# Last head group of the odd layer: VectorE's stick-breaking passes of a step moved directly behind the transposes' copies

## The reference

```python
def _sb_core(q, k, v, qpos, kpos):
    z = jnp.einsum('bqhd,bkhd->bhqk', q, k).astype(jnp.float32) * (SB_HD ** -0.5)
    valid = kpos[None, :] < qpos[:, None]
    log_beta = jax.nn.log_sigmoid(z)
    log_rem = jnp.where(valid, jax.nn.log_sigmoid(-z), 0.0)
    later = lax.cumsum(log_rem, axis=3, reverse=True) - log_rem
    a = jnp.where(valid, jnp.exp(log_beta + later), 0.0).astype(v.dtype)
    return jnp.einsum('bhqk,bkhd->bqhd', a, v)

def _odd_layer(x, pos, caches, prm):
    ...
    q, k, v, g = _split_cols(x @ w_in, (SB_W, SB_W, SB_W, SB_W))
    ...
    o = (o.reshape(b, s, SB_W) * jax.nn.silu(g)) @ w_out
    y = _layernorm(ALPHA * x + o, ln_g, ln_b)
    return y, (k, v)
```

## Time and profile before

| | |
|---|---|
| median of 3 runs | 814.35 us |
| profiled execution | 814.67 us, its span 812.9 us |
| PE busy | 784.4 us, 96% of the span |
| DVE busy | 549.3 us, 68% |
| ACT busy | 393.0 us, 48% |
| POOL busy | 184.9 us, 23% |
| mean granted TensorE clock | 0.995 of full speed |

### The profile page before, as it was taken

How to read it: one execution, slowest core, us unless ns; L and a number is a source line. 1 busy time by engine, 2 the same in 40 slices (tenths; PEclk the granted TensorE clock), 3 DMA queues, 4 the chain that set the end, 5 groups by cost and what they waited for, 6 DMA issues and landing times.

```text
span 812.9 us, 16632 instructions
## 1 busy us (share of the span) xinstructions
PE 784.4 (96%) x6396; PEld 685.5 (84%) x6396; DVE 549.3 (68%) x1087; ACT 393.0 (48%) x903; POOL 184.9 (23%) x262
## 2 busy tenths in 40 slices
PE   6999999999999999999999999999999999999996
PEld 5997799889879987778999998888988888777674
DVE  4576366656677668766933575786577777879778
ACT  3234533444444444431424555765667565677710
POOL 3120010000311232001340142233322343662002
PEclk9999999999999999999999999999999999999998
DMA  7632121211624355414143344334433444444113
GB/s 239 165 102 73 52 61 58 73 34 35 151 66 123 91 121 155 149 54 128 59 125 104 108 116 131 106 106 132 131 107 106 126 118 124 110 129 146 57 40 129
DMA packets 62284, 86.23 MB, mean 106 GB/s; under 512 B 7936, under 2 KB 47648, under 8 KB 62208
## 3 DMA queue, kind: packets, MB, share of 16 engines
q1 hardware_dynamic: 52832, 61.88, 25.3%
q0 software_dynamic: 9376, 23.29, 11.5%
HBM read 74.25 MB, written 10.90 MB: 105 GB/s over the span
## 4 chain that ended last, share of the span: by engine, by line
PE 78%; issue 9%; DVE 7%; ACT 3%; POOL 2%; DMA 1%; SPq 0%; DVEq 0%; ACTq 0%; POOLq 0%
PE turn L1000 27%; PE pair L1000 17%; PE value L1000 14%; PE proj L1000 12%; PE turn L1049 2%; DVE probs L1780 1%; POOL rstd L973 1%; PE turn L1223 1%; PE proj L1049 1%; PE value L1049 1%; PE proj L1223 1%; PE pair L1049 1%; PE value L1223 1%; DVE probs L1776 1%; DMA x_sb<-in_x_prompt_dram 1%
## 5 line engine op out<-in xcount | busy, mean ns | idle before, releaser
L1650 DVE TENSOR_TENSOR w_words<-stage,w_words 128x512 fp32r<-128x512 f32 (+1 forms) x136 | 91.8, 682 | 80.4 <-ACT w_words L1423 80.2
L1000 PE MATMUL turn<-w_words,xT_hi 128*128 128x256 f32 (+2 forms) x664 | 142.5, 311 | 1.0 <-DVE xT_lo L1655 0.7
L1000 PEld LDWEIGHTS turn<-w_words,xT_hi 128*128 128x128 f32 x664 | 107.5, 192 | 6.5 <-DVE x_sb L1912 1.5
L1000 PE MATMUL turn<-w_words,xT_lo 128*128 128x256 f32 (+2 forms) x340 | 102.7, 302 | 0.0
L912 POOL DMA_DIRECT2D k_c<-in_cache_sb_k_dram x128 | 82.6, 653 | 84.0 <-DVE k_cT L1764 79.7
L1423 ACT CAST w_words<-stage 128x512 fp32r<-128x512 f32 (+1 forms) x144 | 87.4, 616 | 27.4 <-DMA stage<-in_w_in_even_dram 12.8
L1000 PE MATMUL turn<-xT_hi,w_words 128*128 128x320 f32 x384 | 90.0, 314 | 0.0
L1000 PE MATMUL value<-w_words,xT_hi 128*128 128x256 f32 (+2 forms) x360 | 79.7, 315 | 1.0 <-DVE w_words L1650 1.0
L1000 PE MATMUL proj<-w_words,xT_hi 128*128 128x256 f32 (+2 forms) x384 | 75.7, 296 | 0.2 <-DVE uq L1856 0.2
L1000 PE MATMUL pair<-w_words,xT_hi 128*128 128x512 f32 (+2 forms) x272 | 71.6, 349 | 0.0
L1000 PEld LDWEIGHTS turn<-w_words,xT_lo 128*128 128x128 f32 x340 | 65.1, 191 | 2.6
(11 more groups left out here) (497 smaller groups left out, 1705.6 us busy)
## 6 DMA issues: line engine op xcount, KB each, us to landing
stage<-in_w_in_odd_dram SPq DMA_DIRECT2D x64, 256.0 KB, 2.8
stage<-in_w_in_even_dram SPq DMA_DIRECT2D x44, 256.0 KB, 2.9
k_c<-in_cache_sb_k_dram POOLq DMA_DIRECT2D x128, 64.0 KB, 2.4
v_c<-in_cache_sb_v_dram SPq DMA_DIRECT2D x32, 256.0 KB, 2.9
mlaK<-in_cache_diff_k_dram POOLq DMA_DIRECT2D x32, 128.0 KB, 4.2
mlaK<-in_cache_diff_v_dram SPq DMA_DIRECT2D x8, 512.0 KB, 5.1
stage<-in_w_out_even_dram SPq DMA_DIRECT2D x16, 256.0 KB, 2.7
stage<-in_w_out_odd_dram SPq DMA_DIRECT2D x16, 256.0 KB, 2.7
```

The source lines that it names most:

```text
L1000: return nc.tensor.matmul(o, l, r, start=first, stop=last)
L1650: v.tensor_tensor(piece(w_lo[:, sec % 2, words]), piece(stage[:, n % STAGES, :]), piece(w_hi[:, sec % 2, words].bitcast(F32)), ALU.subtrac ...
```

## The change

In `stick_pipeline`, for steps of the last group alone, the job `stick` is put directly behind the step's `turn` and `turn2`. Before it stood at the step's end, behind the cached keys, the further bundles, the products of `bsT` and `value`, and `weigh`.

```diff
@@ -159,6 +159,9 @@
                 jobs.append(("turn2", s))
         coming = [("cacheT",) + steps[j] + (k,) for j in samples for k in range(2)
                   if i == max([j - 2, 0] + [n for n in samples if n < j])]
+        early = now[1] == GROUPS - 1
+        if early:
+            jobs.append(("stick", now))
         for bundle in fill[1:]:
             jobs += coming[:1] + bundle
             coming = coming[1:]
@@ -171,7 +174,8 @@
                 later.setdefault(i + turns_on, []).append(job)
         if i >= 1:
             jobs.append(("weigh", steps[i - 1]))
-        jobs.append(("stick", now))
+        if not early:
+            jobs.append(("stick", now))
     return jobs
```

## The result

The changed kernel is slower. Its median over 20 runs is 816.37 us (813.85 to 821.84), beside 813.56 us (811.91 to 815.34) for the kernel before, also 20 runs: ratio 1.0041, interval 1.0027 to 1.0055. The forecast was 811.8 us with a range up to 814.2. It was counted from the median of three runs, 814.35, which lies 0.8 above that of the 20; a gain of 2.6 us was forecast and a loss of 2.8 was measured.

A forecast was written before the change was run, and what follows sets the result against it. TensorE, busy 96% of the span, was taken to lose time only to waits, mainly for late sticks, and its clock. Savings 0.4 + 1.8 + 1.6 + 0.2 - 1.4 = 2.6 us gave 811.8 us; 8-in-10 range 810.4 to 814.2.

The forecast's parts named there:

- Score of B(2,0), saves 0.4: TensorE's 1.19 us wait at this score: the stick of B(3,0) ends earlier, saving 0.38 us; the rest waits for the product.
- Score of B(3,1), saves 1.8: TensorE's 1.82 us wait at this score goes whole, since the stick of B(2,0) starts at 714.9 us.
- Clock, saves 1.6: Six blocks of tile 0, near 725 us: no clock fall, so 4.2 us instead of 5.8; bounds 0 and 1.6.
- Score of BS3, saves 0.2: This score no longer waits about 0.2 us for the stick of BS2, which now stands ahead of other work.
- Key loads, cost 0 (bounds 0 and 1.7): VectorE's key turn waits 0.3 us for BS3's loads without reaching TensorE; at worst 2.0, of which 1.7 would.
- Sums and products in the middle, cost 0: Tile 3's difference and gate products behind sticks still come ahead of TensorE; cost 0, bounds 0 and 1.
- Difference of tile 2, costs 1.4: Near 766 us this difference stands behind two sticks and ends 1.4 us later; TensorE's wait grows from 0.74 to about 2.1.
- slower: the half clock spreads: Rival, 8%: clock falls at new waits before short products; two falls give 816.6 us, three 818.2, old fall not avoided.

The follow-up runs named there:

- e8: Kernel before with only the stick of B(3,0) moved early: 816.76 us, ratio 1.0031 to the kernel before.
- e11: Kernel before with only the stick of B(3,0) early and three GpSimd weight splits beside its scans cut to 16 of 512 columns: 812.66 us, ratio 1.0001.
- e4: Kernel before with only the stick of B(2,0) moved early: 810.67 us, ratio 0.9969 to the kernel before.
- e9: Changed kernel with one more key load on GpSimd, into an unread buffer, at the start of the odd layer: 812.73 us in one execution.
- e1: Changed kernel, all eleven sticks early, with BS3's eight key loads issued by SyncE instead of GpSimd: 814.58 us, ratio 1.0020 to the kernel before.
- e7: Changed kernel with sticks of B(3,0), B(1,1), B(0,0) back at the step's end and BS3's key loads issued by SyncE: 809.57 us, ratio 0.9952 to the kernel before.
- e3: Changed kernel with sticks of B(3,0), B(1,1), B(0,0) back at the step's end, key loads still on GpSimd: 813.97 us, ratio 1.0005 to the kernel before.
- e10: Kernel before with only the sticks of B(1,1) and B(0,0) moved early: 814.25 us, ratio 1.0013 to the kernel before.
- e2: Kernel before, no stick moved, with BS3's eight key loads issued by SyncE instead of GpSimd: 813.01 us, ratio 0.9990.
- e5: Changed kernel with three small loads at the kernel's start issued by SyncE instead of GpSimd: 815.79 us, ratio 1.0033 to the kernel before.

## Why the prediction was wrong

Step by step, as the prediction had them:

- **"Score of B(2,0), saves 0.4"** failed, by the size of one term. The chain was right (stick, half products, value product, score, and the new wait falls on the value product) but the scans were put at 1.17 + 1.8 and took 4.47. Started from 0.98 us earlier, TensorE's value product was due at 708.4 and began at 709.81; the scans' 1.5 us account for it. The number was an average over two unlike instructions of one row of two. e8 and e11 show the cause: alone the stick costs 0.31% and brings the wait of 2.14, with the splits beside it narrowed neither is there. The Trainium skill, page "SBUF — State Buffer", section "Who interferes with whom", has such instructions exclude each other for a whole instruction. The trace agrees in part: scans and splits end by turns, 1.07 to 1.09 us apart, and two splits of each profile took 2.18 to 2.31 us where the third took 1.27. But the first scan of after had run 1.10 us of its 1.17 when the split began, and that it still took 2.29 doesn't follow from such exclusion. By that rule this term was to be about nothing, nearer than mine, and it was worse than nothing, since both scans of the early stick paid in full and before only one did.
- **"Score of B(3,1), saves 1.8"** held: 1.89, and e4 shows it by itself.
- **"Clock, saves 1.6"** held in the profile, 1.63. Against the median it was too much, as far as the clocks of the runs tell: of the 73 runs of the kernel before, 23 have a mean clock of 0.998 and average 812.7, so in about a third of its runs there was no such fall to save, or less of one. e4's 2.5 us, less than 1.8 + 1.6, goes the same way.
- **"Score of BS3, saves 0.2"** held in sign, 0.41.
- **"Key loads, cost 0 (bounds 0 and 1.7)"** failed, and above its upper bound: the two stretches that it delays grew by 2.95. The 1.6 us by which the loads go out sooner look right (1.7) by luck: 0.98 of them came from ahead of the change, and GpSimd's own two splits, from 723.20 to 726.53, held the loads longer than the key turns did (through at 725.99). Wrong was that the stand would come again as long as before. It grew by 2.2, because its end, as the packets show (e9), follows not the issue of the loads but their traffic. VectorE came to the turn at 735.81, as forecast (735.5), and waited 2.81 us where 0.3 and at worst 2.0 were forecast. e1 (keys gone, half of the loss gone) and e7 against e3 (0.53%) show the price.
- **"Sums and products in the middle, cost 0"** isn't contradicted: with the keys by SyncE (e1) TensorE waits for no sum or product of the middle.
- **"Difference of tile 2, costs 1.4"** held: 1.65 in the profile, 1.1 by e10. VectorE's row from the sum to the end of the difference was counted as 6.5 us and took 6.5 (759.81 to 766.31).
- **The rival "slower: the half clock spreads"** had 8%. It put two falls at 816.6 and the median is 816.37, but the nearness is luck. It kept the forecast's waits and the old fall and added two new ones. In the runs of after without half clock (0.997 or more) the time is 814.8, 3.0 above the forecast, so most of the miss is waits, and the median lies 1.6 above these runs. It was weighed by one observation, that 1.19 us at this place had caused none. Of its mechanism the profiles show this: a fall followed the wait of 1.82 in three of three profiles (before, e2, e10), that of 2.14 in one of five (e1), that of 1.6 at tile 2 in one of five (e5), that of 1.6 or 1.7 for the Exp in none of three. So behind the new waits it looks like a matter of chance per run, with another draw for each wait added. That the low runs of after are these same falls is inferred from their clocks; a profile of one was not taken.

One more thing doesn't add up at once. From e7 to e1 the three other sticks are added: that costs 0.68%, where alone they cost 0.31 (e8) and 0.13 (e10). A part of the difference the profile of e8 shows: there B(3,0) gets 0.40 us back at the wait of 1.82, and a fall of the clock less, and with B(2,0) early that wait isn't there to shrink. The rest stays open; half clock behind both new waits in one run would add to it, but no profile shows both.

## What to carry to other kernels

A row that stands for two instructions hides that one was overlapped and the other not: before moving work beside another engine, read the instructions one by one and price each by its own overlap. An engine that gets ahead uncovers the next thing that it waits for, here loads whose last one went out no sooner, so a move that gains is worth trying piece by piece: one stick of eleven brought 0.31%, and all eleven lost 0.41%. And the waits of 1.6 us or more on an otherwise busy TensorE cost more than themselves in part of the runs here, so look at each run's clock and not at one profile. Two profiles of one kernel compare best from the last mark that the change can't have moved.

## What the runs showed of the hardware

- A scan of 128x512 took 1.17 us alone and 2.25 to 2.29 where a GpSimd split of 128x512 lay against it, but once only 1.46 (before). The splits pay as well: of the three of after two took 2.28 and 2.19 us and the last, with no scan beside it, 1.27. VectorE's difference of 128x768, which takes 0.95 or 0.96 us elsewhere in the group in before, took 2.06 there at 718.48 with a split beside it.
- GpSimd's last eight key loads show a stand of 2.35 to 4.54 us before the eighth, unchanged in place by three loads fewer or one more in its queue. It ended 0.9 to 1.3 us after the last packets of the seven. SyncE issued the same eight in 4.38 us without one (e1).
- TensorE's clock fell from 2.4 to 1.2 GHz for part of a stretch behind waits of 1.6 to 2.1 us that stood among short products (0.66 over 725 to 730 in before, 0.67 over 710 to 715 in e1, 0.77 over 770 to 775 in e5), and not behind every wait of that length: none followed in the profiles of after, e8 and e9.
